# Hybrid decoder layer on one core: fused mask, scale and maximum of the attention scores, and later places for three steps

## What is computed

```
h = x @ w_in                      # qa, ka, va, gate_a, qb, kb, vb, gate_b, mg_a, mg_b
s = q @ k.T * dh**-0.5            # banded, causal; masked scores are -inf
m = max(s)                        # branch a: also over the head's sink
p = exp(s - m)
denom = sum(p)                    # branch a: + exp(sink - m)
o = p @ v / denom
y_a = (o_a * silu(gate_a)) @ w_pa # the same for b with w_pb
merged = sigmoid(mg_a + b0) * y_a + sigmoid(mg_b + b1) * y_b
out = layer_norm(2**0.25 * x + merged @ w_out)
```

## Time and profile before

| | |
|---|---|
| median of 3 runs | 1447.14 us (1444.31 to 1447.15) |
| profiled execution | 1442.67 us, its span 1440.9 us |
| TensorE busy | 1405.4 us, 98% of the span |
| VectorE / ScalarE / GpSimd busy | 419.9 / 505.2 / 702.1 us |
| DMA | 140.63 MB, mean 98 GB/s |
| granted TensorE clock | 0.996 of full speed |

### The profile page before, as it was taken

One profiled execution on the slowest core, in us unless ns is written; L12 is line 12 of the kernel. 1 busy time (PEld: TensorE's weight loads), 2 busy tenths in 40 slices (PEclk: granted clock), 3 DMA queues, 4 the chain that ended last, 5 costly groups with the idle time before them and its releaser, 6 DMA issues.

```text
span 1440.9 us, 20261 instructions
## 1 busy us (share of the span) xinstructions
PE 1405.4 (98%) x6692; PEld 1183.4 (82%) x6692; DVE 419.9 (29%) x761; ACT 505.2 (35%) x694; POOL 702.1 (49%) x534
## 2 busy tenths in 40 slices
PE   8999899989999999999999999999999999999996
PEld 7877777778988988898898888888888888888885
DVE  5867667681032213203122111010110101400116
ACT  5454453542343334334234422222222222422122
POOL 4523332354545545454553455454554545564446
PEclk9999999999999999999999999999999999999998
DMA  8422222133333233233332233332333323393322
GB/s 254 122 60 73 58 73 58 55 87 110 94 84 95 75 84 101 62 96 86 93 101 83 62 101 110 93 104 76 100 112 89 108 77 97 99 279 106 95 73 117
DMA packets 191674, 140.63 MB, mean 98 GB/s; under 512 B 17296, under 2 KB 179344, under 8 KB 190736
## 3 DMA queue, kind: packets, MB, share of 16 engines
q1 hardware_dynamic: 191632, 140.08, 33.6%
HBM read 135.82 MB, written 4.19 MB: 97 GB/s over the span
## 4 chain that ended last, share of the span: by engine, by line
PE 85%; DVE 7%; ACT 3%; issue 3%; DMA 1%; POOL 1%; SPq 0%; DVEq 0%; POOLq 0%; ACTq 0%
PE acc L1008 78%; PE ps_out L1088 1%; ACT probs_a L465 1%; PE ps_turn L1062 1%; PE ps_scores L1032 1%; PE ps_out L1079 1%; DVE rowmax L738 1%; DVE probs_a L734 1%; DVE probs_a L768 1%; DVE q_a L725 0%; PE ps_turn L1067 0%; ACT probsT_hi L485 0%; DVE og_hi L792 0%; DMA raw<-w_in 0%; DVE probs_a L733 0%
## 5 line engine op out<-in xcount | busy, mean ns | idle before, releaser
L431 POOL TENSOR_TENSOR w_lo<-raw,w_hi 128x512 fp32r<-128x512 f32 x260 | 342.9, 1319 | 727.2 <-ACT w_hi L458 712.8
L1008 PE MATMUL acc<-x_hi,w_hi 128*128 128x512 f32 x1216 | 480.0, 395 | 0.2 <-POOL w_lo L432 0.2
L1008 PE MATMUL acc<-x_lo,w_hi 128*128 128x512 f32 x1216 | 474.4, 390 | 0.0
L1008 PE MATMUL acc<-x_hi,w_lo 128*128 128x512 f32 x1216 | 474.2, 390 | 0.0
L458 ACT ACTIVATE w_hi<-raw 128x1024 fp32r<-128x1024 f32 x256 | 267.7, 1056 | 446.0 <-PE acc L1008 419.5
L432 POOL TENSOR_TENSOR w_lo<-raw,w_hi 128x512 fp32r<-128x512 f32 x260 | 353.5, 1360 | 0.0
L1008 PEld LDWEIGHTS acc<-x_hi,w_lo 128*128 128x128 f32 x1216 | 228.5, 188 | 48.2
L1008 PEld LDWEIGHTS acc<-x_hi,w_hi 128*128 128x128 f32 x1216 | 228.9, 188 | 44.4 <-POOL w_lo L432 0.6
L1008 PEld LDWEIGHTS acc<-x_lo,w_hi 128*128 128x128 f32 x1216 | 229.0, 188 | 43.7
L1008 PE MATMUL acc<-w_hi,x_hi 128*128 128x384 f32 (+1 forms) x512 | 185.3, 362 | 0.0
L1008 PE MATMUL acc<-w_hi,x_lo 128*128 128x384 f32 (+1 forms) x512 | 185.2, 362 | 0.0
(11 more groups left out here) (165 smaller groups left out, 1120.4 us busy)
## 6 DMA issues: line engine op xcount, KB each, us to landing
raw<-w_in SPq DMA_DIRECT2D x384, 128.0 KB, 2.3
raw<-w_in SPq DMA_DIRECT2D x256, 96.0 KB, 2.5
raw<-w_out SPq DMA_DIRECT2D x128, 128.0 KB, 3.0
raw<-w_in SPq DMA_DIRECT2D x64, 192.0 KB, 2.7
raw<-w_pa SPq DMA_DIRECT2D x64, 128.0 KB, 2.3
raw<-xT SPq DMA_DIRECT2D x8, 512.0 KB, 5.1
raw<-w_in SPq DMA_DIRECT2D x64, 64.0 KB, 2.2
raw<-w_pb SPq DMA_DIRECT2D x64, 64.0 KB, 2.5
```

The costliest lines, as they stand in the source:

```text
L431: nc.gpsimd.tensor_tensor(dst[:, left], raw[:, slot, left], hi[:, left].bitcast(F32), ALU.subtract)
L1008: ins = nc.tensor.matmul(into[:, 0:cols], s, m, start=start and k == 0, stop=stop and k == n - 1)
```

## The change

1. Mask, scale and maximum become one VectorE instruction `tensor_tensor_reduce` (helper `masked`): dst = (scores + mask) x (-scale), and its running minimum, started at 1e30, is the negated maximum. Branch a has two of 128x257 a unit (128x129 for the first block of a tile), branch b one of 128x768. ScalarE's exponential then has a scale of -1.
2. The sinks stand in `ps_scores`, in the column behind each head's scores, written there by `sinks_out`, once for each q tile (4 units); the masks have a column of zeros for them. `mask_b` is stored as 4 x 768 columns instead of 2048 + 256, and `gate_b` lies in another place.
3. The split of q tile 1 moves: ScalarE's `q_high` from the front of block 4 to behind the plan of block 9, VectorE's `split_q(1)` from block 7 to block 10.
4. The split of the first gated tile (j = 0) moves from block 14 to behind the plan of block 15.
5. ScalarE's `high` that stood at block 4 of passes with attention stands at block 5, behind the plan.
6. The first ropes of branch b move from blocks 21, 23, 24 to 23, 24, 25.
7. `scores_ready` waits of the ropes in `iter_a` are merged in front of `sinks_out(0)`.

```diff
-ROPE_PLAN_FIRST = {g + (2 if b[1] == 0 and b[3] < 2 else 1): (b[1], b[3])
+ROPE_PLAN_FIRST = {g + ((4, 3, 2)[b[3]] if b[1] == 0 else 1): (b[1], b[3])
                    for g, b in enumerate(B_BLOCKS) if b[5] and b[1] < 2 and b[3] < 3}
...
-        mask_b = sb("mask_b", [P, NR * SEQ + 2 * P])
+        mask_b = sb("mask_b", [P, NR, SEQ + 2 * P])
...
-        gate_b = sb("gate_b", [P, SEQ])
+        gate_b = at("gate_b", og_at + 23 * 2048, [P, SEQ])
...
-                    e = nc.scalar.activation(s, s, ACT.Exp, bias=negmax[:, buf, hh:hh + 1], scale=A_SCALE,
+                    e = nc.scalar.activation(s, s, ACT.Exp, bias=negmax[:, buf, hh:hh + 1], scale=-1.0,
...
             def attend(kind, plan, g, first_unit, i, between=None):
-                if kind == "a" and g == 4:
-                    q_high(i)
                 for stage, u in plan.get(g, ()):
...
+                if kind == "a" and g == 9:
+                    q_high(i)
...
+                    if with_attention and g == 5:
+                        high(job_a(i), 1 + AHEAD)
...
-                    if opens:
+                    if opens and not (with_attention and g == 4):
                         high(job_a(i), job + AHEAD)
...
+            def masked(dst, scores, mask, scale, least):
+
+                return nc.vector.tensor_tensor_reduce(dst, scores, mask, -scale, -MASKED, ALU.add, ALU.min, least)
+
             def mask_max_a(u, a):
...
-                nc.vector.tensor_copy(probs_a[:, buf, :, 2 * P:2 * P + 1], sink_now[:, 2 * j:2 * j + 2].unsqueeze(2))
-                nc.vector.tensor_tensor(probs_a[:, buf, :, lo:2 * P], ps_scores[:].rearrange("p (h k) -> p h k", h=2)[:, :, lo:2 * P],
-                                        mask_a[:, lo:2 * P].unsqueeze(1).to_broadcast([P, 2, 2 * P - lo]), ALU.add)\
-                    .then_inc(masked_ready, 1)
-                dve.wait_ge(masked_ready, a + 1)
-                nc.vector.tensor_reduce(rowmax[:, buf, :], probs_a[:, buf, :, lo:2 * P + 1], mybir.AxisListType.X, ALU.max)\
-                    .then_inc(rowmax_ready, 1)
-                dve.wait_ge(rowmax_ready, a + 1)
-                nc.vector.tensor_scalar(negmax[:, buf, :], rowmax[:, buf, :], -A_SCALE, None, ALU.mult)\
-                    .then_inc(negmax_ready, 1)
+                dve.sem_inc(scores_seen, 1)
+                for hh in range(2):
+                    last = masked(probs_a[:, buf, hh, lo:2 * P + 1], ps_scores[:, hh * SEQ + lo:hh * SEQ + 2 * P + 1],
+                                  mask_a[:, lo:2 * P + 1], A_SCALE, negmax[:, buf, hh:hh + 1])
+                last.then_inc(negmax_ready, 1)
...
-                if kind == "a" and b == 3:
+                if kind == "a" and b == 3 and j == 1:
                     dve.wait_ge(out_gated, a + 1)
                     split_gated(kind, gate_a[:, j, :], i + A_ITERS * j, i * 2 + j)
...
+            def sinks_out(j, i, maxima):
+
+                if not (isinstance(maxima, int) and maxima == 0):
+                    dve.wait_ge(negmax_ready, maxima)
+                    dve.sem_inc(scores_seen, 1)
+                nc.vector.tensor_copy(ps_scores.rearrange("p (h k) -> p h k", h=2)[:, :, 2 * P:2 * P + 1],
+                                      sink_scaled[:, bass.ds(i * 4 + 2 * j, 2)].unsqueeze(2)).then_inc(sink_set, 1)
+                dve.wait_ge(sink_set, i * 2 + (j + 1))
...
-                if kind == "a" and g == 0:
-                    nc.vector.tensor_copy(sink_now[:], sink_scaled[:, bass.ds(i * 4, 4)]).then_inc(sink_set, 1)
-                    dve.wait_ge(sink_set, i + 1)
...
-                if kind == "a" and g == 7:
+                if kind == "a" and g == 10:
+                    sinks_out(1, i, first_unit + A_UNITS // 2)
                     split_q(1, i * 2)
+                if kind == "a" and g == 15:
+                    dve.wait_ge(out_gated, first_unit + A_UNITS // 2)
+                    split_gated(kind, gate_a[:, 0, :], i, i * 2)
...
                         rope_q(i, 0)
                         if with_attention:
-                            dve.wait_ge(scores_ready, unit_a(i) - A_UNITS // 2)
+                            dve.wait_ge(scores_ready, unit_a(i))
+                        sinks_out(0, i, unit_a(i))
                         split_q(0, i * 2)
                     if A_BLOCKS[g - 1][2:4] == (A_JOBS - 1, 1):
-                        if with_attention:
-                            dve.wait_ge(scores_ready, unit_a(i))
                         rope_q(i, 1)
```

More of the change, by code:

```diff
@@ L180, in build @@
                           for n, where in (("v_hi_a", 8192), ("v_lo_a", 12288)))
-        mask_a = at("mask_a", branch_at + 16384, [P, 2 * P])
-        probsT_lo = at("probsT_lo", branch_at + 17408, [P, 4, P], F32R)
+        mask_a = at("mask_a", branch_at + 16384, [P, 2 * P + 1])
+        probsT_lo = at("probsT_lo", branch_at + 17440, [P, 4, P], F32R)
         probs_a = at("probs_a", shared_at + 6144, [P, 2, 2, 2 * P + 1])
@@ L213, in build @@
         sink_row = sb("sink_row", [P, A_HEADS])
-        sink_scaled, sink_now = sb("sink_scaled", [P, A_HEADS]), sb("sink_now", [P, 4])
-        rowmax, negmax = sb("rowmax", [P, 2, 2]), sb("negmax", [P, 2, 2])
+        sink_scaled = sb("sink_scaled", [P, A_HEADS])
+        negmax = sb("negmax", [P, 2, 2])
         denom, rdenom = sb("denom", [P, 2, 2]), sb("rdenom", [P, 2, 2])
@@ L238, in build @@
         sig_ready, rows_copied = sem("sig_ready"), sem("rows_copied")
-        masked_ready = sem("masked_ready")
-        scores_ready, rowmax_ready, negmax_ready = sem("scores_ready"), sem("rowmax_ready"), sem("negmax_ready")
+        scores_ready, scores_seen, negmax_ready = sem("scores_ready"), sem("scores_seen"), sem("negmax_ready")
         probs_ready, probsT_psum, probsT_ready = sem("probs_ready"), sem("probsT_psum"), sem("probsT_ready")
@@ L470, in exps_b @@
                 act.wait_ge(negmax_ready, a + 1)
-                nc.scalar.activation(probs_b[:], probs_b[:], ACT.Exp, bias=negmax[:, u % 2, 0:1], scale=B_SCALE,
+                nc.scalar.activation(probs_b[:], probs_b[:], ACT.Exp, bias=negmax[:, u % 2, 0:1], scale=-1.0,
                                      accum_out=denom[:, u % 2, 0:1]).then_inc(probs_ready, 1)
@@ L725, in rope @@
                 nc.vector.tensor_tensor(to_order(dst), to_order(dst), from_order(swapped_src), ALU.add).then_inc(rope_done, 1)
+            def masked(dst, scores, mask, scale, least):
+                return nc.vector.tensor_tensor_reduce(dst, scores, mask, -scale, -MASKED, ALU.add, ALU.min, least)
             def mask_max_a(u, a):
-                j, b, buf = *divmod(u, 4), u % 2
-                lo = P if b == 0 else 0
+                lo, buf = P if u % 4 == 0 else 0, u % 2
                 dve.wait_ge(scores_ready, a + 1)
@@ L746, in mask_max_b @@
                 dve.wait_ge(probsT_psum, a)
[L747 to L754, removed]
+                dve.sem_inc(scores_seen, 1)
+                masked(probs_b[:], ps_scores[:, 0:SEQ + 2 * P], mask_b[:, u, :], B_SCALE, negmax[:, u % 2, 0:1])\
                     .then_inc(negmax_ready, 1)
@@ L1223 @@
     dist = in_block[:, None] - np.concatenate([in_block - P, in_block])[None, :]
-    mask_a = np.where((dist >= 0) & (dist < 128), 0.0, MASKED).astype(np.float32)
+    mask_a = np.where((dist >= 0) & (dist < 128), 0.0, MASKED)
+    mask_a = np.concatenate([mask_a, np.zeros((P, 1))], axis=1).astype(np.float32)
     far = t.reshape(NR, P)[:, :, None] - t[None, None, :]
-    near = np.where((far >= 0) & (far <= 128), 0.0, MASKED).transpose(1, 0, 2).reshape(P, NR * SEQ)
+    near = np.where((far >= 0) & (far <= 128), 0.0, MASKED)
     step = p[:, None] - p[None, :]
@@ L1229 @@
     by16 = np.where((step >= 0) & (step % 4 == 0), 0.0, MASKED)
-    mask_b = np.concatenate([near, by4, by16], axis=1).astype(np.float32)
+    mask_b = np.stack([np.concatenate([near[r], by4, by16], axis=1) for r in range(NR)], axis=1).astype(np.float32)
     arrays = {
```

## The result

The changed kernel takes 1429.3 us (median of 4 runs, 1427.57 to 1431.6) against 1445.72 of the kernel before beside it; the ratio is 0.989, 95% interval 0.9867 to 0.9914. It is faster by 1.1%, and by more than the 10 us forecast. The median lies only 0.3 us above the lower end of the range (1429 to 1444), and under the forecast's own range (1433 to 1441). The four took 1427.57, 1428.94, 1429.65 and 1431.6 us, with mean granted clocks of 0.997, 0.996, 0.996 and 0.995.

What follows compares the result with a forecast made beforehand. The chain of one attention unit was taken to set the time; 7.0 us from loop passes, 2.7 from the last pass and 0.8 from the clock make 10.5, said as 10, so 1437 us, range 1429 to 1444.

Steps and rivals of the forecast that it cites:

- the forecast's own range: Whole kernel: 1433 to 1441 us for the forecast itself, without its rivals, chance 0.55.
- values(0): Attention unit 0's value products on TensorE: the 2.4 us wait before them goes in four passes, 9.5 us.
- turn(3): Unit 3's transposes, block 12: wait for a division queued behind the later `q_high`, some 1.7 us, where 0.1 before.
- the ropes: Branch b's first ropes, last pass: moved later, they make TensorE wait for banks, 0.55 to 2.6 us, 1.6 taken.
- turn(5): Unit 5's transposes: wait of 1.2 us (1.6 in the last pass) goes with the later split of gated output.
- the rival in which turn(3) does not wait: Unit 3's transposes: ScalarE's copies or the division fit after all, four waits of 1.7 us less, 1430 us, chance 0.12.
- Fused operation: VectorE's mask, scale and maximum: 0.45 us each, 0.9 a unit, so each maximum comes 0.8 us earlier or more.
- Scores(0): Unit 0's score products: 0.1 to 0.2 us later per pass, from a sink copy between tile 0's rope and split.
- Gated split: VectorE's split of gated output, moved behind unit 5's maximum: no wait before that unit's transposes, 0.6 us at most.
- Clock: First pass, near 90 us: the dip of the granted clock goes with the stall before it, 0.8 us more gained.
- The rival of a lower clock behind the new waits: New waits bring the clock down, each dip 0.8 to 1.8 us; 1441 us with three and contended ropes, chance 0.18.
- `mask_b`: Branch b's mask load: grows by a third, from 8.0 to about 10.7 us, and costs nothing.

Runs made afterwards that it cites:

- e7: The change with job 5's weight copy of the last pass made at block 8 instead of block 9: 1425.91 us, ratio 0.988.
- e1: The change with all moves undone, leaving the fused operation, sinks in PSUM and merged waits: 1422.24 us, ratio 0.9846.
- e9: The change with old places for all but `q_high` (behind block 8) and `split_q(1)` (block 10): 1417.8 us, ratio 0.9828.
- e8: The change with `q_high` behind block 8 and job 10's weight copy held until branch b's three q ropes are done: 1418.42 us, ratio 0.9826.
- e4: The change with branch b's ropes at their old blocks 21, 23, 24: 1427.67 us, ratio 0.9885.
- e6: The change with ScalarE's weight copy back at block 4: 1430.43 us, ratio 0.9905.
- e3: The change with `q_high` one block earlier, behind block 8 instead of 9: 1420.96 us, ratio 0.9835.
- e2: The kernel before with the moves alone, mask, maximum and scale still four operations: 1448.93 us, ratio 1.0037.
- e5: The change with `q_high` behind block 8 and branch b's ropes at their old blocks: 1418.87 us, ratio 0.9829.

## Why the prediction was right, and where its sizes were off

The mechanism was right in its main steps (the wait at values(0) gone, a new one at turn(3), waits for the ropes) and the total short: 15.2 us instead of 10.5 by the terms, in the same span. One cause was misread, that of turn(5). That the time still fell into the range is partly luck: its lower end stood for the rival in which turn(3) does not wait, and turn(3) waited; and what was counted too low in the passes was partly offset by what was counted too low against the last pass.

- **Values(0):** gone in all passes. The step of products over this wait was 2.77 us, where the usual one is 0.23, so it was worth 2.54, not the 2.4 of the waits view.
- **Waits as a view shows them.** This is the largest error, some 1.2 us a pass. The view counts a wait from the modelled end of the last product (0.39 us long), while products start every 0.23 us. Each wait before a product is therefore worth 0.16 to 0.17 us more than its row, and waits shorter than that are not shown. In the second pass, by starts of the same products in both traces: values(0) 2.54, turn(5) 1.41, turn(6) 0.44, turn(7) 0.42, turn(2) 0.13, and single steps longer by 0.06 to 0.11, most of them right behind a wait, against 1.42 more at turn(3). That is 3.97, where the terms gave 2.3. The 1.17 us by which "busy" fell fits such tails (four waits in the view, turn(2) and the small steps).
- **Fused operation:** 0.34 from start to start and 0.42 in all, against 0.45 taken (0.34 to 0.88 the bounds): two took 0.7, not 0.9. Rate and source were those of the row chosen: from 257 to 768 columns it grows from 420 to 958 ns, 1.05 ns a column, and the additions grow from 418 ns at 256 to 687 at 512, the same. The Trainium skill (Vector Engine (DVE) Microarchitecture Reference, Points that are easy to get wrong) states half rate for the two-source form with two sources in SBUF that are not bf16. Here one source lies in PSUM and the rate is full; no run has both in SBUF.
- **Turn(3):** 1.36 us waited, 1.7 forecast; the two fused operations are 0.2 of the difference. The last pass had 3.15: the sum left out that the division comes 0.6 us behind a weight copy there, and e7 shows that this alone is the 1.7 us.
- **Scores(0):** no later, where 0.15 a pass was forecast. In the second pass the rope's sum in front of it started later and took 1.23 us instead of 1.59; as before, it ends 0.5 us behind a GpSimd subtraction. The next copy starts 0.1 us behind the sum's end in both kernels, although the sink copy (0.15) now lies between them.
- **Gated split:** turn(5) waits no more, as forecast, but the cause was misread: e1 and e9 have the split in the old place and no wait either. The earlier maximum of the fused version is enough; in e1 the split even still stands beside GpSimd (0.63 + 1.57 us).
- **Ropes:** 0.88 + 1.74 us, the upper end (0.9 + 1.7), and e8's 0.36 is near the lower (0.55). The middle (1.6) was the wrong choice. By the rule of the Trainium skill (SBUF — State Buffer, Who interferes with whom) it was 2.6; this trace agrees (1.62, 1.59, 1.15, 1.59 us for 0.7 each).
- **Clock:** the dip of the first pass is gone; that pass gained 1.26 us more than the second, 0.8 forecast. (By the row, 0.74 over 6.5 us, the lower level lasted 3.4 us, not 3.7.) The rival of a lower clock behind the new waits did not come true in the profiled execution, but e4 and e6 show it behind the same wait at turn(3).
- **`mask_b`:** with a third more bytes it landed in 7.9 us; 10.7 were taken. TensorE does not wait for it in either kernel.
- Per stage: 5.2 against 3.1 in the first pass, 4.0 against 2.3 in the next two, 1.3 against 2.7 in the last stretch, and 0.7 in the prologue, which no step explains: it starts with transfers, and 0.9 to 2.7 us of wait for their splits are seen there from run to run.

The prediction did not see that the moves, weighed together, cost. It priced `q_high` at 1.7 us against 2.4 won at values(0), of which e1 leaves 0.9 once the operation is fused: a move was credited with what the fused operation mostly does alone. All of the moves together cost 6.3 us on top of it (e1 against the change), and the fused version without them is 21.4 us under the kernel before.

## What to carry to other kernels

Price each part of a change on top of the others: when one part shortens a chain, the waits that another part was meant to remove may be gone already, and only its cost is left. Where an instruction of one engine is put in front of another's by a wait, add up what stands behind the waiting one; moving the awaited copy by one block was worth 6 us (e3). In a stream of overlapping products count waits from start to start.

## What the runs showed of the hardware that was not expected

- The clock fell to 1.2 GHz for 3.4 us behind some waits and not behind equal ones. Before: one of four waits of 2.4 us before values(0). The change: none, though turn(3) waits 3.15 us; e4 and e6: behind that same wait of 3.15 us. e2: one of three waits of 2.82 us, and the one of 4.53. In the prologue TensorE waits for its first splits: behind waits of 2.3 to 2.4 us it fell each time (e3, e5, e6, e8), behind those of 0.9 to 2.1 us it did not (the other seven profiles). A fall cost 1.2 to 1.7 us in the passes and the stretch (first pass before and in e2, e4, e6). What decides is open; none of the runs tells it.
- It differs between executions of one kernel too: three of e6's four took 1430.4 to 1430.8 us with a mean clock of 0.995, the fourth 1427.56 with 0.997. Kernels with a wait of 2.4 us or more in attention spread over 1.8 to 6.5 us, those without over 0.5 to 1.5.
- VectorE's division of two SBUF-to-SBUF multiplies, 0.62 us, took 2.31 beside two GpSimd subtractions. GpSimd's own subtraction stretched from 1.29 to 1.74 us beside the ropes. By these rows the two engines take turns, and both lose.
- The fused operation's read of its accumulator is a row of its own, 83 ns, and the next operation starts with it (152.64 in both rows): it costs nothing in between.
